# A decoder step's diagonal recurrence, taken over pairs of tokens

## The reference, cut to what matters

```python
def s5_scan(u, s0_re, s0_im, ...):            # u: (B, T, 512), 32 groups of 16 channels
    dt = jnp.exp(log_dt)[:, None]
    mag = jnp.exp(a_re * dt)
    abar = mag * (cos(a_im * dt) + i sin(a_im * dt))      # one complex factor per (group, state)
    bbar = ((abar - 1) / a) * (b_re + i b_im)
    bu = einsum('btgc,gnc->btgn', u, bbar)                # complex, 64 states per group
    s_t = abar * s_{t-1} + bu_t                           # along the tokens
    y = einsum('btgn,gcn->btgc', re(s), c_re) - einsum('btgn,gcn->btgc', im(s), c_im) + d_skip * u
    z = gelu(y)
    return z * sigmoid(z @ w_glu + b_glu), re(s[:, -1]), im(s[:, -1])
```

## Time and profile before

| | us |
|---|---|
| median of 3 runs | 2353.83 |
| lowest, highest | 2350.49, 2356.2 |
| profiled execution, its span | 2353.7 |
| TensorE matmul busy in it | 2044.5 |
| VectorE busy | 1177.2 |
| ScalarE busy | 650.0 |
| GpSimd busy | 1001.2 |

### The profile page before, as it was taken

One profiled execution on the slowest core, in us unless ns is written; L12 is line 12 of the kernel. 1 busy time (PEld: TensorE's weight loads), 2 busy tenths in 40 slices (PEclk: granted clock), 3 DMA queues, 4 the chain that ended last, 5 costly groups with the idle time before them and its releaser, 6 DMA issues.

```text
span 2353.7 us, 38380 instructions
## 1 busy us (share of the span) xinstructions
PE 2044.5 (87%) x14289; PEld 1496.2 (64%) x14289; DVE 1177.2 (50%) x3447; ACT 650.0 (28%) x977; POOL 1001.2 (43%) x874
## 2 busy tenths in 40 slices
PE   9889999999997667889898889999999986777777
PEld 4554899999995323334356346999999973233332
DVE  2554699423333533578456834997233333333333
ACT  1332244545551001112134022454555520000000
POOL 0111469830004565656514303688500026666665
PEclk9899999999998798999997989999999998888878
DMA  6473434444447999999932334244444469999998
GB/s 233 173 279 119 144 129 159 161 162 162 168 163 264 331 355 369 362 329 335 350 122 62 90 116 152 81 161 153 162 168 164 165 217 348 360 346 357 365 357 312
DMA packets 179914, 529.91 MB, mean 225 GB/s; under 512 B 22066, under 2 KB 49234, under 8 KB 179474
## 3 DMA queue, kind: packets, MB, share of 16 engines
q0 software_dynamic: 87296, 310.68, 36.3%
q1 hardware_dynamic: 91282, 216.25, 26.8%
q10 hardware_dynamic: 1152, 0.52, 0.1%
HBM read 524.69 MB, written 2.69 MB: 224 GB/s over the span
## 4 chain that ended last, share of the span: by engine, by line
PE 68%; another core or an unknown queue 8%; DVE 8%; POOL 5%; issue 5%; DMA 3%; ACT 2%; SPq 1%; DVEq 0%; ACTq 0%; PEldq 0%
PE bank L950 10%; PE bank L952 10%; PE bank L951 10%; PE bank L769 8%; PE bank L1014 8%; PE bank L990 4%; POOL u_low L703 3%; PE bank L1032 3%; PE bank L1092 2%; DVE i_one_hot L2172 2%; DMA v_slot<-in_peer_v,v_rows 2%; POOL v_slot L712 2%; PE bank L979 1%; PE bank L1242 1%
## 5 line engine op out<-in xcount | busy, mean ns | idle before, releaser
L712 POOL DMA_INDIRECT v_slot<-in_peer_v,v_rows x417 | 394.6, 946 | 703.8 <-PE bank L952 441.1
L950 PE MATMUL bank<-h_parts,u_high 128*128 128x288 f32 x2048 | 607.0, 296 | 7.9 <-POOL u_low L703 6.2
L951 PE MATMUL bank<-h_parts,u_high 128*128 128x288 f32 x2048 | 604.4, 295 | 0.0
L952 PE MATMUL bank<-h_parts,u_low 128*128 128x288 f32 x2048 | 602.8, 294 | 0.0
L950 PEld LDWEIGHTS bank<-h_parts,u_high 128*128 128x128 f32 x2048 | 384.1, 188 | 11.6 <-POOL u_low L703 9.6
L952 PEld LDWEIGHTS bank<-h_parts,u_low 128*128 128x128 f32 x2048 | 385.8, 188 | 0.0
L951 PEld LDWEIGHTS bank<-h_parts,u_high 128*128 128x128 f32 x2048 | 384.6, 188 | 0.0
L1597 ACT CAST u_high<-u_slot 128x1024 fp32r<-128x1024 f32 x256 | 268.7, 1050 | 400.5 <-PE bank L952 249.1
L703 POOL TENSOR_TENSOR u_low<-u_slot,u_high 128x1024 fp32r<-128x1024 f32 x120 | 321.1, 2686 | 93.5 <-ACT u_high L1597 93.4
L1014 PE MATMUL bank<-v_slot,weight_columns 128*32 128x512 f32 x1412 | 274.1, 687 | 57.3 <-DMA v_slot<-in_peer_v,v_rows 34.1
L1014 PE MATMUL bank<-v_slot_of_columns,weight_columns 128*32 128x512 f32 x636 | 246.2, 687 | 69.8 <-DVE weight_columns L2179 44.0
(11 more groups left out here) (393 smaller groups left out, 2463.2 us busy)
## 6 DMA issues: line engine op xcount, KB each, us to landing
u_slot<-in_peer_ut SPq DMA_DIRECT2D x256, 512.0 KB, 3.5
w_q<-in_peer_w_q SPq DMA_DIRECT2D x8, 2048.0 KB, 14.4
region<-in_cache_a_kt SPq DMA_DIRECT2D x8, 960.0 KB, 11.8
region<-in_cache_a_v SPq DMA_DIRECT2D x8, 960.0 KB, 11.4
v_slot<-in_peer_v,v_rows POOLq DMA_INDIRECT x417
region<-in_ev_w_in SPq DMA_DIRECT2D x3, 2048.0 KB, 15.1
region<-in_pool_kv POOLq DMA_DIRECT2D x40, 128.0 KB, 5.0
ckv_t_norm<-in_pool_ckv SPq DMA_DIRECT2D x64, 64.0 KB
```

Source lines behind the costliest of these rows:

```text
L712: pool.indirect_dma_start(out=VS[l][slot], out_offset=None, in_=v_rows, in_offset=bass.IndirectOffsetOnAxis(ap=IDX[:, at:at + 1], axis=0)) ...
L950: pe.matmul(bank, uh, HR[:, 0, c, :], start=(c == 0), stop=False)
L951: pe.matmul(bank, uh, HR[:, 1, c, :], start=False, stop=False)
L952: ins = pe.matmul(bank, ul, HR[:, 0, c, :], start=False, stop=(c == KC - 1))
```

## The change

For pairs of tokens the recurrence is s_{2n+1} = abar^2 s_{2n-1} + (abar bu_{2n} + bu_{2n+1}). So the scan runs over 128 pairs with the factor mag^2 (par[14]), the turn table E has 128 entries of twice the angle, and the input of a pair comes from two matmuls into one bank, with a stepped input matrix (LB, transposed BT1) for the even token and the old one for the odd. The states of odd tokens come out of the scan. The output of an even token is made from the state one pair before, through the stepped output matrix CL, and from the token's own input through K0 (the product of the output and the input matrix). ScalarE writes UT with the even tokens first and the odd ones behind (`inputs_of_states`), and the last products put the order back. All sums of products are made on VectorE; `turned_sums` is gone. BU, XR and T12 have half the size, places of their own for each quarter, and some waits go with that. The output matrix CBD is loaded in layer 0. The orders of TensorE and VectorE are written anew.

```diff
@@ SyncE
+                    sp.wait_ge(sem("v_used"), 48)
+                    load(CBD, I["s5_c"], "gain0_then_s5_par_loaded")
                     sp.wait_ge(sem("s5_factors_made"), 3)
...
-                sp.wait_ge(sem("ut_ready"), 4)
-                load(CBD, I["s5_c"], "x_then_odd_loaded1")
...
-                sp.wait_ge(sem("quarter_ready"), 2)
                 pages_of(sp, CKPT[4], I["pool_ckv"][:, :, 0:P], 4, "latents_loaded1")
...
-                sp.wait_ge(sem("quarter_ready"), 4)
+                sp.wait_ge(sem("quarter_ready"), 5)
+                sp.wait_ge(sem("sd_scores"), 2)
+                sp.wait_ge(sem("bu_ready"), 36)
                 for n in range(2):
                     load(W_OUT1[n], ...)
@@ GpSimd and ScalarE: the wait for quarter_ready 2 ahead of their pages of CKPT[5], [6], [7] goes
@@ TensorE
                 def turn_inputs():
-                    pe.wait_ge(sem("s5_factors_made"), 2)
-                    for k in range(2):
-                        bank = to_act()
+                    pe.wait_ge(sem("s5_factors_made"), 4)
+                    for b in (BSC, LB):
+                        for k in range(2):
+                            bank = to_act()
...
+                    bank = to_act()
+                    for g in range(4):
+                        for q in range(4):
+                            ins = mm(bank[32 * q:32 * q + 32, 32 * g:32 * g + 32], [(BSC[:, k, 4 * g + q, :], CBD[:, k, 4 * g + q, :]) for k in range(2)])
+                    ins.then_inc(a_full, 1)
...  states_in
-                            pe.matmul(bank[:, 0:SEQ], BT[rows, k, g, :], UT[rows, g, 0:SEQ], ...)
+                            mm(bank[:, 0:PAIRS], [(BT1[rows, k, g, :], UT[rows, g, 0:PAIRS]), (BT[rows, k, g, :], UT[rows, g, PAIRS:SEQ])])
...  states_out
-                        parts = ((0, XR2[g % 2][0]), (0, XR2[g % 2][1]), (1, BU[g][:, 0]), (1, BU[g][:, 1]))
-                        ins = mm(bank[rows, 0:SEQ], [(CBD[:, k, 4 * g + q, :], part[:, q, :]) for k, part in parts])
+                        now = (XR[g][0], BU[g][:, 0])
+                        mm(bank[rows, PAIRS:SEQ], [(CBD[:, k, 4 * g + q, :], now[k][:, q, :]) for k in range(2)])
+                        pe.matmul(bank[rows, 0:PAIRS], K0[rows, g, :], UT[rows, g, 0:PAIRS], start=True, stop=False, ...)
+                        for k in range(2):
+                            ins = pe.matmul(bank[rows, 1:PAIRS], CL[:, k, 4 * g + q, :], now[k][:, q, 0:PAIRS - 1], start=False, ...)
...  order
                 latent_scores(0)
                 states_in(2)
                 sample_states_out()
-                turned_sums(0)
                 latent_turn(0)
-                turned_sums(1)
+                states_in(3)
                 latent_values(0)
                 states_out(0)
-                states_in(3)
                 latent_out_turn(0)
+                latent_scores(1)
                 states_out(1)
-                turned_sums(2)
-                turned_sums(3)
-                latent_scores(1)
+                latent_turn(1)
                 states_out(2)
-                latent_turn(1)
+                latent_values(1)
                 states_out(3)
-                latent_values(1)
                 latent_out_turn(1)
@@ VectorE
+            def s5_steps(k):
+                f = [bc(par[11], 2, 32), bc(par[12], 2, 32)]
+                if k == 0:
+                    cmul([LB[:, 0], LB[:, 1]], f, [BSC[:, 0], BSC[:, 1]], ...)
+                else:
+                    dve.wait_ge(sem("gain0_then_s5_par_loaded"), 48)
+                    TS(CBD[:, 1], CBD[:, 1], -1.0, None, ALU.mult)
+                    cmul([CL[:, 0], CL[:, 1]], f, [CBD[:, 0], CBD[:, 1]], ..., conj=True)
+                    say("s5_factors_made")
...  in the groups q of layer 0, n = q - 42
-                        if 0 <= n < 20:
+                        if 0 <= n < 20 and n % 10 < 8:
                             s5_turns(n // 10, n % 10)
+                        if n == 18:
+                            s5_steps(0)
...
+                        if n == 26:
+                            s5_steps(1)
...  states_products
-                    say("products_ready")
                     step(dve.scalar_tensor_tensor(out=re, in0=sin, scalar=-1.0, in1=re, op0=ALU.mult, op1=ALU.mult))
                     settle()
-                    say("products_ready")
+                    step(dve.tensor_tensor(out[0], out[0], im, ALU.add))
+                    step(dve.tensor_tensor(out[1], out[1], re, ALU.add))
+                    settle()
...  states_scan
-                                step(dve.tensor_tensor_scan(T12[k][:, q, :], par[7]... .broadcast_to([P, SEQ]), bank[...], 0.0, ALU.mult, ALU.add))
+                            step(dve.tensor_tensor_scan(T12[g % 2][k][:, q, :], par[14]... .broadcast_to([P, PAIRS]), XR[g][k][:, q, :], 0.0, ALU.mult, ALU.add))
...  states_turn_back, behind the four products
+                    step(dve.tensor_tensor(now[0], now[0], XR[g][1], ALU.add))
+                    step(dve.tensor_tensor(now[1], now[1], BU[g][:, 1], ALU.add))
                     settle()
                     say("quarter_ready")
+                    for k in range(2):
+                        step(dve.tensor_copy(LASTP[:, k, 4 * g:4 * g + 4], now[k][:, :, PAIRS - 1]))
...  order
                 latent_scores(0)
                 states_products(0)
                 out_of_sample_states()
-                states_products(1)
                 states_scan(0)
                 states_turn_back(0)
+                states_products(1)
                 states_scan(1)
                 latent_out(0)
                 states_turn_back(1)
                 out_of_states(0)
                 latent_out_turned(0)
+                latent_scores(1)
                 states_products(2)
+                states_scan(2)
                 out_of_states(1)
+                states_turn_back(2)
                 states_products(3)
-                states_scan(2)
-                states_turn_back(2)
                 states_scan(3)
-                latent_scores(1)
                 out_of_states(2)
                 states_turn_back(3)
+                latent_out(1)
                 out_of_states(3)
-                latent_out(1)
                 latent_out_turned(1)
                 for m in range(4):
                     dve.wait_ge(sem("sgm_ready"), m + 1)
-                    TT(OT1[:, m, :], ZG[:, m, :], SGM[:, m, :], ALU.mult)
+                    (the same for the 256 prompt tokens, with the pairs put back in order, and then for the 32 sample tokens)
@@ ScalarE
-                            copy_out(BU[g][:, k, q, :], full()[:, 0:SEQ], "bu_ready")
+                            copy_out(BU[g][:, k, q, :], full()[:, 0:PAIRS], "bu_ready")
+                def inputs_of_states(m):
+                    bank = full()
+                    link(act.copy(UT[:, m, 0:SEQ].rearrange("p (j n) -> p n j", j=2), bank[:, 0:SEQ].rearrange("p (n j) -> p n j", j=2)))
+                    copy_out(UT[:, m, SEQ:NT], bank[:, SEQ:NT], "ut_ready")
```

More of the change, by code:

```diff
@@ L315, in take @@
                 return v
-        E = [tile_at(f"s5_turns{hf}", [2, SG2, SEQ], HB[hf]) for hf in range(2)]
+        E = [tile_at(f"s5_turns{hf}", [2, SG2, PAIRS], HB[hf]) for hf in range(2)]
+        LB = tile_at("s5_b_stepped", [2, SCH, 32], HB[1] + 2048)
+        STEP_TMP = tile_at("s5_step_tmp", [2, SCH, 32], HB[1] + 3072)
+        BT1 = tile_at("s5_b_stepped_t", [2, 4, P], HB[1] + 3072)
+        CBD = tile_at("s5_c", [2, SCH, 32], HB[0] + 2048)
+        CL = tile_at("s5_c_stepped", [2, SCH, 32], HB[0] + 3072)
         E_TMP = tile_at("s5_turns_tmp", [2, SG2, P], HB[2] + 2048)
@@ L400, in build @@
         BT = end.take("s5_b_t", 2, 4, P)
-        end.at += 256
+        K0 = end.take("s5_c_times_b", 4, 32)
+        end.at += 128
         LASTP = end.take("s5_last_prompt", 2, SCH)
@@ L1346, in states_in @@
                             bank = to_act()
-                            pe.matmul(bank[:, 0:SEQ], BT[rows, k, g, :], UT[rows, g, 0:SEQ], start=True, stop=True).then_inc(a_full, 1)
+                            mm(bank[:, 0:PAIRS], [(BT1[rows, k, g, :], UT[rows, g, 0:PAIRS]), (BT[rows, k, g, :], UT[rows, g, PAIRS:SEQ])]).then_inc(a_full, 1)
                 def turn_queries_keys(t):
@@ L1456, in latent_out_turn @@
                     pe.transpose(bank[:, 0:P], OSD, ident).then_inc(d_full, 1)
-                def turned_sums(g):
-                    for k in range(2):
-                        pe.wait_ge(sem("products_ready"), 2 * g + k + 1)
-                        parts = (XR2[g % 2][k], BU[g][:, 1 - k])
-                        for h in range(2):
-                            bank = to_dve()
-                            for n, part in enumerate(parts):
-                                ins = pe.matmul(bank[:, :].rearrange("p (q n) -> p q n", n=SEQ), ident, part[:, 2 * h:2 * h + 2, :],
-                                                start=(n == 0), stop=(n == 1))
```

(24 more changed lines are left out.)

62 lines of the change are left out of this document (34 added, 28 removed).

## The result

Over 20 runs of each, the kernel before takes 2347.31 us in the median and the changed one 2355.8: 1.0035 times as long, 95% interval 1.0022 to 1.0048, which is 8.2 us slower (5.2 to 11.3). Measured again on another chip, the changed kernel is 1.0032 (1.0015 to 1.0049). The direction was forecast, and the stall was where the prediction put it. Of the 12.2 us between 2368 and 2355.8, 6.5 come from the base: the three runs shown (2353.83) lay that far above the median of twenty. The other 5.8 are the terms of the sum.

The account below looks back on a forecast made before the run. VectorE's recurrence was taken to bound 1290 to 1369 us, with SyncE's page queue deciding the forecast. Terms 9.7 + 2.3 + 2.0 = +14.0 us on 2353.7 gave 2367.7, so 2368, range 2359 to 2377.

Parts of the forecast that it names:

- the stall: Odd layer: VectorE reaches latent_scores(1) early and stands 34 us, TensorE with it, until SyncE's latent pages land.
- the base: Time before the change to which the terms were added: 2353.7 us for the execution, 2353.83 for the runs' median.
- the end of layer 0: +2.0 us (-2 to +4.5): removed s5_turns work 0 to -2, s5_steps at group 68 +1, CBD load +1.
- A quarter: Recurrence on VectorE, 4 of 16 state chunks: from 15.8 to 11.3 us, saving 18 us over four.
- Behind the pages, +9.7: Odd layer after the latent pages land: last quarter ready 14.0 us later, tail 4.3 us shorter, net +9.7.
- the tail: From the last quarter's signal through glu and last products: 5.3 us gained, 1.0 lost, net gain 4.3.
- Entry, +2.3: Start of the odd layer: in_columns(0) waits for a bank ScalarE frees, +3.1; shorter ScalarE copies, -0.8.
- The prediction's other +1: End of layer 0: CBD's 512 KB load between gathers, 1.5 us if seen in full, taken as 1.
- The fast one: Rival: pages are there when VectorE comes, so no wait; 2331 us, 7 in 100.
- The milder wait: Rival: the wait comes, but entry and layer 0 cost nothing; 2361 to 2363 us, 12 in 100.
- its second condition: Part of the milder wait: states_out and the second round also run at a higher clock, giving 2357 us.
- The queue: SyncE's page issue, 1.07 us a page, sets when pages land; by the skill's sentence it would hardly matter.

Follow-up runs that it names:

- e1: Changed kernel with the second round's latent pages issued ahead of value pages on SyncE and GpSimd: 2338.67 us, 0.9968 of before.
- e2: Changed kernel with the second round of sample scores back in its old place, on VectorE behind the scans of quarter 3: 2344.31 us, 0.9986 of before.
- e5: Kernel before, full-sized tiles, with latent_scores(1) moved ahead of products(2) on VectorE and ahead of states_out(1) on TensorE: 2371.69 us, 1.0117 of before.
- e7: Changed kernel with three unused 1024-element VectorE products put back at each of the four steps s5_turns lost: 2362.92 us, 1.0081 of before.
- e14: The changed kernel as it is, measured again on the other chip: 2273.19 us, 1.0032 of before.
- e11: Kernel before with the four last steps of s5_turns cut to one copy each, without their two squarings: 2261.54 us, 0.9977 of before.
- e13: Kernel before with both gather-phase edits, e11's copies and e12's added products: 2265.55 us, 0.9998 of before.
- e8: Kernel before without the four last steps of s5_turns, two memsets a half at the first step instead: 2350.22 us, 1.0022 of before.
- e12: Kernel before with six 512-element VectorE products added at group 60 and six at group 68 of layer 0's second gather phase: 2274.23 us, 1.0031 of before.
- e4: Changed kernel with second-round scores behind all four quarters, glu and gate ahead of that round's exponential, plus e1's page order: 2329.77 us, 0.9926 of before.
- e9: Kernel of e4 with turn_inputs split, so in_columns(0) follows the first two banks: 2251.71 us, 0.9932 of before.

## Why the prediction was off, and what of it was right

The measured time lies below the range, with the mechanism as forecast. Two steps failed: the base, taken from three runs (6.5 us), and the term for the end of layer 0, put at +2.0 (4.5 of the other 5.8 us). The points follow the prediction's terms.

- *What bounds the kernel, and the stall.* Right. VectorE was forecast at latent_scores(1) 26 us behind the start of products(0); it took 25.0 (1282.65 to 1307.61), and the wait is 35.31 us (34 forecast). The scores start 96.2 us behind the first page's issue (96.4 forecast). e1, e2 and e5 show it from three sides: pages earlier, scores later, and the same order in the old kernel.
- *A quarter.* Right: products 1361.46 to 1365.44 = 4.0; eight scans 2.7 with their wait, 3.0 forecast; the last turn back to its signal 3.9, 4.0 forecast. The 128-element scan has a mean of 403 ns and 0.33 us from start to start. The prediction's estimate from the Trainium skill, 424 ns ("VectorE: DVE Perf Modes", TRN2 errata), lies 5% above the 403; back to back, where 0.33 us counts, it is nearly 0.1 too long.
- *Behind the pages, +9.7.* Right in size. The first pair of profiles has +10.9; over more of them it is 147.7 (changed, e7, e14) less 139.2 (before, e11 to e13) = +8.5, or +9.2 if e8 (135.7), whose code is the same here, is counted with the old ones. In the first pair the last quarter comes 13.4 us later against the first page (14.0 forecast), and the tail gains 2.5 (4.3 forecast). states_out(1) took 4.1 us (1347.10 to 1351.2), 4.2 forecast, but states_out(3) 5.9, as its matmuls go from 0.41 to 0.63 us a pair on the way (1373.24, 1376.06), and glu 9.07 instead of 8.00. These 2.8 us go with the granted clock (third column from the right): it fell to 0.50 over the end of states_out(3) and the start of glu, where glu had 1.00 in the kernel before. From the end of glu to the out projection it is 5.4 us for 5.3, so the last products cost 0.1 more and not the 1.0 forecast. The changed kernel, then the one before:

```profile
1375.00:1381.50 6.50, 6.50 (x31) 3.81 (x31) 0.77 (x2) 0.44 (x1) 0.00 (x0) 0.50 1.00 350
1379.00:1387.00 8.00, 8.00 (x34) 6.04 (x34) 0.29 (x1) 1.36 (x2) 0.00 (x0) 1.00 0.46 159
```

- *Entry, +2.3.* Over seven profiles of changed and six of old kernels 63.55 - 61.34 = +2.2. in_columns(0) came 3.04 us later against the first bank (3.97 for 0.93), 3.1 forecast. The cause was half right: one wait for ScalarE is 0.86 us of it, the rest is TensorE's own added work, the stepped banks and the small products. The 128-column copies took 0.27 us as expected.
- *End of layer 0, +2.0: the step that failed.* The whole leaves less than nothing for it: +8.2 less 10.7 for the other stages is -2.5 (-5.5 to +0.6 by the interval of the times alone, and -3.2 with e8 counted above), and again 7.3 less 9.9 on the other chip. The gather phase is 299.7 us in the mean of three old kernels and 296.2 in five changed ones, -3.5, little beyond their scatter. I had priced the removed steps at 0 to -2, as covered by TensorE, and the added ones at 0 and 1, 3 at most. Taken singly both lie outside these bounds, in opposite directions: removing gives 5.2 us (e11), adding costs 7.0 (e12), that is 0.36 and 0.84 us for each us of work, and 0.7 in e7. Together they come to -0.5 (e13), where the prediction had +1: the two wrong prices nearly cancel, and that the term was off by 4.5 us and not by more is luck. The earlier trace rows warned: VectorE is busy 34.67 of 40 us between 1080 and 1120. My reading is that each group passes through VectorE and TensorE both, so that "TensorE is on the chain" does not make VectorE free; e8, slower with less work, does not fit it. The prediction's other +1, for the 512 KB of CBD, was not tried alone. What takes the changed kernels from e13's -0.5 to about -3 stays open.
- *The base.* 6.5 us of the miss are three runs taken for the median. The spread of this kernel's runs is 2340.5 to 2357.5, and the range of 18 us was built on the step from before to after alone.
- *Rivals.* The fast one, 22.6 us faster, did not come, by its own condition: pages at 1336 or earlier. e4 makes the condition true in another order, and is 17.4 us faster. The milder wait, +3 to +9 us on its base, is where the measured +8.2 lies, and half for its own reason: layer 0 cost nothing, but the entry did. A higher clock behind the pages, its second condition, did not come.
- *The queue.* The Trainium skill's sentence that several issuing engines save only time that is usually small ("DMA: Bandwidth & Descriptors", "Issuing engines are not separate DMA queues") would have made e1 worthless. e1 is worth 16 us by order alone, at a DMA share of 0.34: here the issue, 1.07 us a page, is the cost. It is not small beside the transfer, whose pages land 1.9 us after their issue.

## What to carry to other kernels

Before counting what an engine saves, ask what it meets when it arrives early: here 18 us of saved VectorE time and a reordering ended in a wait for pages that one sequencer issues at its own pace. Order the queue by who needs what first, then put the work that needs no page ahead of the work that does; this turned 8 us slower into 17 faster with the same arithmetic. And do not put work on a busy second engine at nothing because another engine is on the chain: try each edit alone, as two wrong prices can cancel in the sum.

## What was not expected of the hardware

- While TensorE stood for 34.5 us its granted clock was 0.50 (1.2 GHz), and it was 0.50 in the stage ahead of it too, where TensorE was busy 20.59 of 24 us with short matmuls. The same two matmuls of states_out take 0.38 to 0.41 us at 1347 and 0.64 at 1361, after 8.72 us of idling.
- ScalarE's copy that takes pairs apart (256 elements with a stride) takes 0.61 us against 0.37 for a plain one. I had counted on the plain price; here it is hidden beside matmuls of 4 us. VectorE's last products, which put 256 elements back in order, take 0.43 us, a plain one of this size 0.42. ScalarE in order of time in the changed kernel:

```profile
1190.70 0.61 ACT L1743 COPY s_in<-bank 128x256 f32<-128x256 f32 x1 [2.24 <-PE bank L775]
```

- The same kernel before runs 3.5% faster where e9 to e14 ran than where e1 to e8 did (2266 against 2345 us). There the gather phase takes 268 to 280 us instead of 294 to 309, and what follows the start of the out projection 915 instead of 955 to 961, while the stages of the odd layer differ by 4 us at most. From 870 to 1150 us, within the gather phase, the DMA engines moved 377 to 389 GB/s there and 338 to 362 where e1 to e8 ran, at a DMA share of 0.93 and more in both. A time is only good beside runs of the same chip.
